# Matrix-memory heads of a two-block network: low parts in the other 64 rows, scores as two rounded products

## The chip, the cores and the metric

The kernel runs on one core of a Trainium2 chip. The metric is the time of one execution on the device in microseconds (us); the time given is the median of the runs shown. The engines are PE (TensorE; PEld is its weight load), DVE (VectorE), ACT (ScalarE), POOL (GpSimd) and SP (SyncE).

## The reference, cut to what matters

Two transformer-like blocks run one after the other on 512 tokens of width 1024. The change lies in the second block, in the matrix-memory heads (mLSTM) of its mixer. There are M_HEADS = 4 heads, with queries and keys of M_DK = 64 and values of M_DV = 128 features:

```python
u_c = jax.nn.silu(causal_dwconv(u, conv_w, conv_b))
u_h = u_c.reshape(Bn, S, M_HEADS, M_DV)
q_m = jnp.einsum('bshd,hde->bhse', u_h, wq_m)      # 64 features a head
k_m = jnp.einsum('bshd,hde->bhse', u_h, wk_m)
...
qk = jnp.einsum('bhcjd,bhcsd->bhcjs', qc, kc) * Dw  # scores times decay
num = (... + jnp.einsum('bhcjs,bhcse->bhcje', qk, vc))
den = (... + jnp.sum(qk, axis=-1))
h = num / jnp.maximum(jnp.abs(den), jnp.exp(-m_j))[..., None]
...
return jnp.concatenate([y_m, y_a], axis=-1) @ w_out
```

The other half of the mixer, y_a, is a causal attention over low-rank queries and keys ("latent attention"), which the kernel runs right behind the heads.

## The kernel before

All engines have programs of their own, written out by hand in the order in which they run; semaphores tie them together. Large products (a "panel" is a group of output columns) are computed from rounded parts: each f32 operand is a rounded high part and a rounded low part of type fp32r, and three rounded products (high·high, high·low, low·high) go into one PSUM bank (lines 410, 486, 2585, 2569). POOL and ACT split the weights (lines 3257, 3265, 1446), a panel ahead of PE. PE's banks 0 to 3 go round: before PE writes block `blk` it waits until the semaphore acc_free has counted block `blk - 4` as read out.

The heads take their place in this order. In the second block PE computes the low-rank panel L_low, then four blocks in which it makes queries and keys of one head each (line 2585, three products of 512 columns: rows 0 to 63 of the bank are the queries, rows 64 to 127 the keys, one column a token), then the value panel L_vb (line 486). ACT copies each bank out in two copies of 64 rows (lines 2713 and 2714), into QM and KM in f32, two heads to a tensor, the even head in the upper 64 rows and the odd head in the lower. The second copy frees the bank. Then ACT goes on with squares, root and scaling of the low-rank tensors (2438, 2444, 2450, 2452), and DVE with its part of them (2457 and 2459).

A head's scores are taken over all 128 rows, since its keys share their tensor with the neighbour head's. So the queries must be zero in the neighbour's 64 rows: POOL makes Q_PADDED with four multiplications by a column mask (`heads_query_pool`, line 2919), between the last weight split ahead of it and `memory_pool`. While it does, DVE computes the gate rows of 4 partitions (`gate_rows_dve`, lines 2397 to 2402), for whose end PE waits at line 2625.

The scores themselves (`mlstm_qk_pe`, line 2649): for key block bs of 0 to 3 (128 keys), PE multiplies the keys with the queries of tokens bs·128 to 511, that is 512, 384, 256 and 128 columns, as one f32 product, which the trace shows as two passes. The results alternate between two banks. DVE multiplies each with its decay block E (line 2795, `ml["w"]`), and PE may write score block u only when DVE has done block u - 2. Between the pairs of blocks PE runs the value products of the head before (line 2663) and the broadcast of the decay row of the head after the next (line 2672); DVE runs the additions of the mask (2678) and the outputs (2804 to 2813). After head 3 comes the latent attention (line 1599), which has products over 128 and over 64 rows.

## Time and profile before

| | |
|---|---|
| median of 3 runs | 1868.13 us (1868.02 to 1868.85) |
| span of the profiled execution | 1866.1 us |
| PE busy | 1836.2 us, 98% |
| PEld busy | 1552.8 us, 83% |
| POOL busy | 1367.8 us, 73% |
| DVE busy | 920.0 us, 49% |
| ACT busy | 756.6 us, 41% |

The profiled execution gives times within its span; the rest of the time, 2.0 us against the median, lies around it. The busy shares are means over many stages. Start times below are from the span's start: the heads' queries and keys are made at 1230 us, the scores at 1304 to 1324 us.

### The profile page before, as it was taken

To read this page: it belongs to the slowest core of one execution; us is meant where nothing else is said; L and a number is where in the kernel's file an instruction comes from. 1 tells how busy PE (TensorE), PEld (TensorE's weight loads), DVE (VectorE), ACT (ScalarE), POOL (GpSimd) and SP (SyncE) were. 2 spreads that over 40 slices of the span, in tenths; PEclk is the share of its full clock that TensorE was granted. 3 is DMA by queue.
4 is the path that set the end of the run, shared out by engine and by line. 5 is a ranking of instruction groups with operands and counts; after the bars stand their busy time and mean duration, and the time that the engine had idled before them with its cause. 6 is when DMAs were issued, how large, how long until landed. Compare 5 with 4: busy or idle time off the path is not lost.

```text
span 1866.1 us, 26050 instructions
## 1 busy us (share of the span) xinstructions
PE 1836.2 (98%) x9519; PEld 1552.8 (83%) x9519; DVE 920.0 (49%) x1806; ACT 756.6 (41%) x1459; POOL 1367.8 (73%) x1211
## 2 busy tenths in 40 slices
PE   7999999999999999999999999999999999999999
PEld 6888888888878888888888888897679988888887
DVE  5677777772117885455403411727664465203410
ACT  4577777764027773242101210567644532001200
POOL 8766666698854558989888988763345589888885
PEclk9999999999999999999999999999999999999999
DMA  7322222223333232422333333222023223432342
GB/s 223 113 69 68 68 69 68 69 68 91 91 114 89 52 86 91 160 68 90 90 105 98 90 93 110 69 63 68 24 68 114 91 68 90 110 93 90 94 109 68
DMA packets 213612, 165.69 MB, mean 89 GB/s; under 512 B 14478, under 2 KB 209873, under 8 KB 213122
## 3 DMA queue, kind: packets, MB, share of 16 engines
q1 hardware_dynamic: 208134, 149.32, 27.3%
q10 hardware_dynamic: 5372, 14.98, 2.4%
q8 instruction: 64, 1.05, 0.2%
q14 instruction: 42, 0.34, 0.1%
HBM read 161.11 MB, written 7.37 MB: 90 GB/s over the span
## 4 chain that ended last, share of the span: by engine, by line
PE 57%; POOL 3%; issue 2%; DVE 2%; ACT 2%; POOLq 0%; ACTq 0%; DVEq 0%
PE bank L410 44%; PE bank L486 4%; POOL w_lo L3265 2%; PE bank L436 1%; PE bank L1599 1%; POOL w_hi L3257 1%; PE bank L3014 1%; PE bank L1623 1%; PE bank L1821 1%; PE bank L1800 1%; PE bank L1810 0%; PE bank L2663 0%; PE bank L1609 0%; PE bank L429 0%; POOL x_features L761 0%
## 5 line engine op out<-in xcount | busy, mean ns | idle before, releaser
L3265 POOL TENSOR_TENSOR w_lo<-w_raw,w_hi 128x512 fp32r<-128x512 f32 (+1 forms) x572 | 721.7, 1294 | 197.9 <-ACT w_hi L1446 188.4
L3257 POOL TENSOR_TENSOR w_hi<-w_raw,one 128x512 fp32r<-128x512 f32 (+1 forms) x428 | 440.8, 1061 | 213.6 <-PE bank L410 193.9
L410 PE MATMUL bank<-h_hi,w_hi 128*128 128x512 f32 x952 | 376.8, 396 | 0.8 <-POOL w_lo L3265 0.6
L410 PE MATMUL bank<-h_hi,w_lo 128*128 128x512 f32 x952 | 371.8, 391 | 0.0
L410 PE MATMUL bank<-h_lo,w_hi 128*128 128x512 f32 x952 | 371.1, 390 | 0.0
L410 PE MATMUL bank<-a_hi,w_hi 128*128 128x512 f32 x832 | 325.8, 392 | 0.4 <-DVE a_lo L553 0.3
L410 PE MATMUL bank<-a_hi,w_lo 128*128 128x512 f32 x832 | 324.0, 389 | 0.0
L410 PE MATMUL bank<-a_lo,w_hi 128*128 128x512 f32 x832 | 323.7, 389 | 0.0
L410 PEld LDWEIGHTS bank<-h_hi,w_lo 128*128 128x128 f32 x952 | 178.6, 188 | 38.9
L410 PEld LDWEIGHTS bank<-h_hi,w_hi 128*128 128x128 f32 x952 | 178.9, 188 | 35.6 <-issue 1.4
L410 PEld LDWEIGHTS bank<-h_lo,w_hi 128*128 128x128 f32 x952 | 179.0, 188 | 33.5
L410 PEld LDWEIGHTS bank<-a_hi,w_hi 128*128 128x128 f32 x832 | 156.2, 188 | 33.0 <-issue 0.6
L410 PEld LDWEIGHTS bank<-a_hi,w_lo 128*128 128x128 f32 x832 | 156.1, 188 | 32.8
L410 PEld LDWEIGHTS bank<-a_lo,w_hi 128*128 128x128 f32 x832 | 156.3, 188 | 31.5
L2174 ACT ACTIVATE arena<-bank 128x512 f32<-128x512 f32 x64 | 38.0, 597 | 319.7 <-PE bank L410 312.9
L2195 DVE TENSOR_TENSOR a_lo<-arena,a_hi 128x512 fp32r<-128x512 f32 x64 | 81.6, 1275 | 156.5 <-ACT a_hi L2166 156.5
L486 PE MATMUL bank<-w_hi,h_hi 128*128 128x256 f32 (+1 forms) x448 | 129.4, 289 | 0.2
L486 PE MATMUL bank<-w_lo,h_hi 128*128 128x256 f32 (+1 forms) x448 | 126.5, 282 | 0.0
L486 PE MATMUL bank<-w_hi,h_lo 128*128 128x256 f32 (+1 forms) x448 | 126.4, 282 | 0.0
L1140 DVE SCALAR_TENSOR_TENSOR arena<-bank,cols,arena 128x510 f32<-128x510 f32 (+1 forms) x128 | 95.6, 747 | 7.7 <-ACT arena L1124 4.3
L486 PEld LDWEIGHTS bank<-w_hi,h_hi 128*128 128x128 f32 x448 | 85.9, 192 | 1.2 <-DVE a_free_hi L2340 0.6
L486 PEld LDWEIGHTS bank<-w_hi,h_lo 128*128 128x128 f32 x448 | 85.9, 192 | 0.3 <-issue 0.2
(506 smaller groups left out, 3012.6 us busy)
## 6 DMA issues: line engine op xcount, KB each, us to landing
w_raw<-in_w_ff SPq DMA_DIRECT2D x32, 1024.0 KB, 5.4
w_raw<-in_w_in SPq DMA_DIRECT2D x31, 1024.0 KB, 5.4
w_raw<-in_w_mlp_in SPq DMA_DIRECT2D x16, 1024.0 KB, 5.3
w_raw<-in_w_mlp_out SPq DMA_DIRECT2D x16, 1024.0 KB, 5.7
w_raw<-in_w_in SPq DMA_DIRECT2D x26, 512.0 KB, 4.1
w_raw<-in_w_ssd_out SPq DMA_DIRECT2D x8, 1024.0 KB, 5.6
bias_rows<-bias_row ACTq DMA_DIRECT2D x1, 4096.0 KB, 15.1
w_raw<-in_w_attn_out SPq DMA_DIRECT2D x4, 1024.0 KB, 5.3
```

Source lines behind the costliest of these rows:

```text
L410: mm = pe.matmul(bank[:, 0:ntok], a, b[:, koff + k, 0:ntok], start=(k == 0 and n == 0), stop=(k == L.kb - 1 and n == 2))
L436: mm = pe.matmul(banks[blk % 4][:], a, b[:, koff + k, :], start=(k == 0 and n == 0 and not ready_high), stop=(k == L.kb - 1 and n == len(p ...
L486: mm = pe.matmul(banks[blk % 4][:, t * width:(t + 1) * width], a[:, k, tok], b, start=(k == 0 and n == 0), stop=(k == L.kb - 1 and n == 2))
L1140: ins = dve.scalar_tensor_tensor(dst[:, lo:hi], src[:, lo + s:hi + s], colv(f"conv_w{k}", conv_column(g, b)), dst[:, lo:hi], ALU.mult, ALU ...
L1599: mm = pe.matmul(score_bank[n % 2][:, 0:w["n"]], qT, kT, start=(i == 0), stop=(i == len(w["q"]) - 1))
L1623: mm = pe.matmul(value_bank[:, 0:dv], mem[1][n % 2][:, j * P:(j + 1) * P], w["v"][j], start=(j == 0), stop=(j == nb - 1))
L1800: mm = pe.matmul(scores_of[:, 0:(k1 - k0) * P], QS[g % 2][:, r, n * P:(n + 1) * P], KS[g % 2][:, part, k0 * P:k1 * P], start=(part == 0), ...
L1821: mm = pe.matmul(value_bank[:], VSTACK[g % 2][:, k0 + j, :], part[:, j, :], start=(j == i == 0), stop=(j == k1 - k0 - 1 and i == 1))
L2174: act.activation(RL[b % 2], acc(L1, b), ACT.Relu).then_inc(ml_relu, 1)
L2195: dve.tensor_tensor(a_lo[:, b, :], SQR[b % 2], a_hi[:, b, :].bitcast(F32), ALU.subtract).then_inc(ml_lo, 1)
L3257: pool.tensor_tensor(w_hi[:, slot, part], raw[:, slot, part], one[:].broadcast_to([P, n]), ALU.mult).then_inc(split_hi, 1)
L3265: ins = pool.tensor_tensor(w_lo[:, slot, part], raw[:, slot, part], w_hi[:, slot, part].bitcast(F32), ALU.subtract)
```

## The change

The heads' queries and keys are kept rounded, with their low parts beside them. QUERIES and KEYS hold one head to a slice of 128 rows. In an even head QUERIES has the rounded queries in the upper 64 rows and their low part in the lower; KEYS has the rounded keys in both halves; the low part of the keys lies in the upper rows of LOW_ROWS. In an odd head the roles of queries and keys are exchanged, and the upper and lower rows of LOW_ROWS with them. ACT makes three copies a head instead of two, DVE two subtractions from the bank, and DVE's second one frees the bank. A score block is then two rounded products into one bank: the first over 128 rows (high·high and one high·low at once), the second over 64 rows (the other one). POOL's four multiplications and the semaphore `padded` go. ACT gets a wait for acc_free ahead of the first read of L_vb.

```diff
-        QM = A(0, 1024).rearrange("p (b s) -> p b s", b=2)
-        KM = A(1024, 1024).rearrange("p (b s) -> p b s", b=2)
+        QUERIES = arena_rounded[:, 0:2048].rearrange("p (h s) -> p h s", h=M_HEADS)
+        KEYS, LOW_ROWS = moving[:, 0:M_HEADS, :], moving[:, M_HEADS:M_HEADS + 2, :]
+        TOP, BOTTOM = slice(0, 64), slice(64, P)
...
-        Q_PADDED = a_free_hi[:, 0:M_HEADS, :]
...
+        def heads_high_act(act, h):
+            bank = banks[(L_low.b0 + T // 2 + h) % 4]
+            act.wait_ge(acc_ready, L_low.b0 + T // 2 + h + 1)
+            if h % 2 == 0:
+                copies = ((QUERIES[TOP, h, :], bank[TOP]), (KEYS[BOTTOM, h, :], bank[BOTTOM]), (KEYS[TOP, h, :], bank[BOTTOM]))
+            else:
+                copies = ((KEYS[BOTTOM, h, :], bank[BOTTOM]), (QUERIES[TOP, h, :], bank[TOP]), (QUERIES[BOTTOM, h, :], bank[TOP]))
+            for dst, src in copies:
+                ins = act.activation(dst, src, ACT.Copy)
+            ins.then_inc(ml["high"], 1)
+
+        def heads_low_dve(dve, h):
+            bank = banks[(L_low.b0 + T // 2 + h) % 4]
+            q_low, k_low = ((QUERIES[BOTTOM, h, :], LOW_ROWS[TOP, h // 2, :]), (LOW_ROWS[BOTTOM, h // 2, :], KEYS[TOP, h, :]))[h % 2]
+            dve.wait_ge(ml["high"], h + 1)
+            dve.tensor_tensor(q_low, bank[TOP], QUERIES[TOP, h, :].bitcast(F32), ALU.subtract)
+            dve.tensor_tensor(k_low, bank[BOTTOM], KEYS[BOTTOM, h, :].bitcast(F32), ALU.subtract).then_inc(acc_free, 1)
...
         def mlstm_qk_pe(pe, h, part):
-            pe.wait_ge(ml["padded"], h + 1)
+            if h == 0 and part[0] == 0:
+                pe.wait_ge(acc_free, L_low.b0 + T // 2 + M_HEADS)
...
-                pe.matmul(QK_RING[u % 2][:, 0:S - bs * P], KM[:, h // 2, bs * P:(bs + 1) * P], Q_PADDED[:, h, bs * P:S],
-                          start=True, stop=True).then_inc(ml["qk"], 1)
+                dst, keys = QK_RING[u % 2][:, 0:S - bs * P], slice(bs * P, (bs + 1) * P)
+                if h % 2 == 0:
+                    low = LOW_ROWS[TOP, h // 2, keys], QUERIES[TOP, h, bs * P:S]
+                else:
+                    low = KEYS[BOTTOM, h, keys], LOW_ROWS[BOTTOM, h // 2, bs * P:S]
+                pe.matmul(dst, KEYS[:, h, keys], QUERIES[:, h, bs * P:S], start=True, stop=False)
+                pe.matmul(dst, *low, start=False, stop=True).then_inc(ml["qk"], 1)
...
             for h in range(M_HEADS):
-                act.wait_ge(acc_ready, L_low.b0 + T // 2 + h + 1)
-                p0 = 64 * (h % 2)
-                act.activation(QM[p0:p0 + 64, h // 2, :], acc(L_low, T // 2 + h, 0, 64), ACT.Copy)
-                act.activation(KM[p0:p0 + 64, h // 2, :], acc(L_low, T // 2 + h, 64, P), ACT.Copy).then_inc(acc_free, 1)
+                heads_high_act(act, h)
             low_rank_squares_act(act, [(4, 128, CKT[:, :, 0:128]), (8, 64, CKT[:, :, 128:192])])
             low_rank_root_act(act)
+            act.wait_ge(acc_free, L_vb.b0)
...
             conv_dve2(dve)
+            for h in range(M_HEADS):
+                heads_low_dve(dve, h)
             low_rank_dve(dve)
...
-        def heads_query_pool(pool):
-            pool.wait_ge(acc_free, L_low.b0 + T // 2 + M_HEADS)
-            pool.wait_ge(lt["turn"], 6)
-            pool.wait_ge(lt["red"], 4 * T)
-            for h in range(M_HEADS):
-                rows = (m_lt[:, 64:65], m_gt[:, 63:64])[h % 2].bitcast(F32)
-                pool.tensor_tensor(Q_PADDED[:, h, :], QM[:, h // 2, :], rows.broadcast_to([P, S]), ALU.mult).then_inc(ml["padded"], 1)
...
-                    heads_query_pool(pool)
                     memory_pool(pool)
```

On ACT, at the place where the banks of the four heads are read out, this stood before (arena stands for QM and KM):

```order
L2424 ACTIVATE arena<-bank,small 128x192
L2713 ACTIVATE arena<-bank 64x512 [waits acc_ready]
L2714 ACTIVATE arena<-bank 64x512
L2713 ACTIVATE arena<-bank 64x512 [waits acc_ready]
L2714 ACTIVATE arena<-bank 64x512
```

And this stands there now (arena_rounded is QUERIES, decay_moving is KEYS and LOW_ROWS):

```order
L2444 ACTIVATE arena<-bank,small 128x192
L2381 ACTIVATE arena_rounded<-bank 64x512 [waits acc_ready]
L2381 ACTIVATE decay_moving<-bank 64x512 x2
L2381 ACTIVATE decay_moving<-bank 64x512 [waits acc_ready]
L2381 ACTIVATE arena_rounded<-bank 64x512 x2
```

Each head has one copy more, and none of the three frees the bank. On DVE, behind the convolution of the second block, these rows are now between the last split of the convolution and the reciprocal of the low-rank part, which stood next to each other before:

```order
L2231 TENSOR_TENSOR a_lo<-arena,a_hi 128x512 [waits sp_hi,ms_uc] x2
L2389 TENSOR_TENSOR arena_rounded<-bank,arena_rounded 64x512 [waits ms_high]
L2390 TENSOR_TENSOR decay_moving<-bank,decay_moving 64x512
L2389 TENSOR_TENSOR decay_moving<-bank,arena_rounded 64x512 [waits ms_high]
L2390 TENSOR_TENSOR decay_moving<-bank,decay_moving 64x512
```

The second subtraction of a head frees its bank. On PE, heads 0 and 1 of the scores read like this before (2672 is the broadcast of the decay row, 2663 a value product):

```order
L2672 MATMUL bank<-arena,ident 128x512
L2649 MATMUL bank<-a_free_hi,arena 128x512 [waits ms_padded]
L2649 MATMUL bank<-a_free_hi,arena 128x384
L2649 MATMUL bank<-a_free_hi,arena 128x256 [waits ms_w,ms_padded]
L2649 MATMUL bank<-a_free_hi,arena 128x128 [waits ms_w]
L2672 MATMUL bank<-arena,ident 128x512 [waits ms_exp]
L2649 MATMUL bank<-a_free_hi,arena 128x512 [waits ms_w,ms_padded]
L2649 MATMUL bank<-a_free_hi,arena 128x384 [waits ms_w]
L2663 MATMUL bank<-arena 128x129 [waits ms_w,lt_kept]
```

And now:

```order
L2698 MATMUL bank<-arena,ident 128x512
L2675 MATMUL bank<-arena_rounded,decay_moving 128x512 [waits acc_free]
L2676 MATMUL bank<-arena_rounded,decay_moving 128x512
L2675 MATMUL bank<-arena_rounded,decay_moving 128x384
L2676 MATMUL bank<-arena_rounded,decay_moving 128x384
L2675 MATMUL bank<-arena_rounded,decay_moving 128x256 [waits ms_w]
L2676 MATMUL bank<-arena_rounded,decay_moving 128x256
L2675 MATMUL bank<-arena_rounded,decay_moving 128x128 [waits ms_w]
L2676 MATMUL bank<-arena_rounded,decay_moving 128x128
L2698 MATMUL bank<-arena,ident 128x512 [waits ms_exp]
```

Each f32 product has become a product over 128 rows (2675) and one over 64 (2676) into the same bank; the rest of PE's order is the same.

## Rows read from the trace of the kernel before

**Rows 1.** The page: span, and busy time of each engine with its share.
```profile
span 1866.1 us, 26050 instructions
PE 1836.2 (98%) x9519; PEld 1552.8 (83%) x9519; DVE 920.0 (49%) x1806; ACT 756.6 (41%) x1459; POOL 1367.8 (73%) x1211
```

**Rows 2.** Busy time by stretches: PE, PEld, DVE, ACT, POOL, clock, DMA.
```profile
1304.20:1323.79 19.59, 18.33 (x97) 12.87 (x96) 12.96 (x41) 12.45 (x41) 0.00 (x0) 1.00 0.00 1
1300.00:1866.00 566.00, 557.46 (x2809) 460.40 (x2807) 218.34 (x432) 155.38 (x341) 397.78 (x326) 1.00 0.28 84
```

**Rows 3.** Timeline, making of queries and keys (PE): start, duration, instruction.
```profile
1232.94 0.39 PE L2585 MATMUL bank<-a_hi,w_lo 128*128 128x512 f32 x1
1233.16 0.28 PE L486 MATMUL bank<-w_hi,h_hi 128*128 128x256 f32 x1
1233.28 0.28 PE L486 MATMUL bank<-w_hi,h_lo 128*128 128x256 f32 x1
```

**Rows 4.** Timeline, the same place on ACT, and where its part ends.
```profile
1231.30 0.59 ACT L2713 ACTIVATE arena<-bank 64x512 f32<-64x512 f32 x1
1231.91 0.60 ACT L2714 ACTIVATE arena<-bank 64x512 f32<-64x512 f32 x1
...
1242.85 1.27 ACT L2452 ACTIVATE arena<-arena,latent_stats 128x128 f32<-128x128 f32 x4
```

**Rows 5.** Groups by shape, DVE: busy us, mean ns; idle before.
```profile
L2195 DVE TENSOR_TENSOR a_lo<-arena,a_hi 128x512 fp32r<-128x512 f32 x64 | 81.6, 1275 | 156.5 <-ACT a_hi L2166 156.5
L1852 DVE TENSOR_TENSOR a_hi<-bank,a_hi 64x512 fp32r<-64x512 f32 x16 | 11.0, 689 | 5.5 <-ACT a_hi L1843 5.1
L2231 DVE TENSOR_TENSOR a_lo<-arena,a_hi 128x512 fp32r<-128x512 f32 x4 | 2.7, 685 | 0.8 <-ACT a_hi L2226 0.8
```

**Rows 6.** Timeline, POOL's padded copies and the gate rows on DVE.
```profile
1287.43 1.21 DVE L2397 TENSOR_TENSOR_SCAN a_free_lo<-a_free_hi,cmask 4x512 f32<-4x512 f32 x1
1288.68 1.35 DVE L2398 TENSOR_TENSOR a_free_lo<-a_free_lo 4x512 f32<-4x512 f32 x1
1290.06 1.95 DVE L2399 TENSOR_TENSOR_SCAN arena<-a_free_lo 4x512 f32<-4x512 f32 x1
1293.42 1.15 DVE L2401 TENSOR_SCALAR arena<-arena 4x512 f32<-4x512 f32 x1
...
1288.39 1.09 POOL L2919 TENSOR_TENSOR a_free_hi<-arena,m_lt 128x512 f32<-128x512 f32 x1 [3.39 <-PE bank L2545]
1292.81 1.48 POOL L2919 TENSOR_TENSOR a_free_hi<-arena,m_gt 128x512 f32<-128x512 f32 x1
```

**Rows 7.** Weight loads of PE around its wait for the gate rows.
```profile
1293.61 0.19 PEld L486 LDWEIGHTS bank<-w_lo,h_hi 128*128 128x128 f32 x1
1294.73 0.32 PEld L2625 LDWEIGHTS bank<-ident,a_free_lo 4*128 4x128 f32 x4 [0.93 <-issue]
```

**Rows 8.** Timeline of the scores: weight loads, PE and DVE.
```profile
1304.63 0.19 PEld L2649 LDWEIGHTS bank<-a_free_hi,arena 128*128 128x128 f32 x1 [0.24 <-issue]
1305.06 0.19 PEld L2649 LDWEIGHTS bank<-a_free_hi,arena 128*128 128x128 f32 x1 [0.24 <-issue]
...
1304.83 0.69 DVE L2678 TENSOR_TENSOR a_free_lo<-bank,a_free_lo 128x512 f32<-128x512 f32 x1 [6.48 <-PE bank L2672]
1305.76 1.20 DVE L2795 SCALAR_TENSOR_TENSOR arena<-bank,arena 128x512 f32<-128x512 f32 x2 [0.24 <-PE bank L2649]
...
1316.26 0.89 PE L2649 MATMUL bank<-a_free_hi,arena 128*128 128x256 f32 x4 [0.44 <-DVE a_free_hi L2795]
...
1320.73 1.03 PE L2663 MATMUL bank<-arena,a_free_hi 128*128 128x129 f32 x6 [0.51 <-ACT a_free_lo L2763]
```

**Rows 9.** Weight loads in the latent attention, 128 and 64 rows in turn.
```profile
1358.92 0.30 PEld L1599 LDWEIGHTS bank<-a_free_lo,a_free_hi 128*128 128x128 f32 x2
1359.98 0.29 PEld L1599 LDWEIGHTS bank<-a_free_lo,a_free_hi 64*128 64x128 f32 x2 [0.76 <-issue]
1361.04 0.14 PEld L1609 LDWEIGHTS bank<-ident,a_free_hi 128*128 128x128 f32 x1 [0.76 <-issue]
```

More of the change, by code:

```diff
@@ L2281, in build_program @@
         MEMB = A(2048, 2048)
-        ml = {k: sem("ms_" + k) for k in ("gates", "rows", "rows_in", "conv", "uc", "qk", "act", "dve", "pe", "arg", "exp", "w", "num", "out", "sq", "inverse", "padded", "bc", "head", "ss", "root")}
+        ml = {k: sem("ms_" + k) for k in ("gates", "rows", "rows_in", "conv", "uc", "qk", "act", "dve", "pe", "arg", "exp", "w", "num", "out", "sq", "inverse", "high", "bc", "head", "ss", "root")}
         lt = {k: sem("lt_" + k) for k in ("ang", "sin", "table", "ss", "root", "inverse", "low", "kr", "red", "qn", "kn", "turn", "kept")}
```

## The prediction

> **What bounds the kernel now.** First the page: PE is busy 98% of 1866.1 us, and no other engine more than 83% [rows 1]. Then the busy time by stretches: from 1300 us to the end PE has 557.46 of 566 us, so what reaches PE's order ahead of that stays in the end time nearly one for one [rows 2]. PE's granted clock is 1.00 in both stretches, the level of 2.4 GHz. The question is therefore only: by how much does each edit move PE? Three places can: where the heads' banks are read out (1231 us), where PE waits for DVE's gate rows (1294 us), and the scores (1304 to 1324 us), where PE is busy 18.33 of 19.59 us [rows 2].
>
> **Place 1, the banks.** Before, PE goes from the last product of the heads (start 1232.94) to the first one of L_vb (1233.16) with no gap; a product of 512 columns lasts 0.22 us from start to start [rows 3]. That first product of L_vb must wait until the bank of head 0 is free. ACT starts on it at 1231.30 and frees it with its second copy at 1231.91 + 0.60 = 1232.5, 0.65 us ahead of the need [rows 4]. Now ACT makes three copies of the same shape at 0.61 us from start to start: 1231.30 + 2 × 0.61 + 0.59 = 1233.1. Then DVE subtracts twice. The trace has a subtraction of this kind, 64 rows by 512, one operand in a bank and one in SBUF: 0.689 us [rows 5]. Two in a row take about 0.60 + 0.69 (the pair of decay products, 1.20 us for 512 and 384 columns, shows such an overlap [rows 8]). DVE is free there; the bank is free at 1233.1 + 0.1 + 1.3 = 1234.5. PE waits from 1233.16 to 1234.5: **+1.35 us**. Bounds: 0 would need subtractions that start before the copies end, which their order excludes; +2.6 if each subtraction takes 1.28 us, as the one with both operands in SBUF does beside POOL [rows 5]. I take 1.35, since the nearest row has the same shape and operand places. The banks of heads 1 to 3 are asked for one 5.8-us block later each, or are never late.
>
> ACT's four extra copies are 2.45 us, less the 1.35 us by which PE is later too. Queued behind them are squares, root and scaling of the low-rank part, whose end releases PE's transposes at 1250 us. That end is at 1242.85 + 1.27 = 1244.1 [rows 4]; even 2.5 us more leaves over 3 us. DVE's reciprocal waits for ACT's root, so the 5 us of subtractions are done long before. ACT's added wait for all four banks is over at about 1240.0, while ACT gets to it at about 1243. All three cost nothing as long as that slack stands.
>
> **Place 2, POOL's copies go.** They run from 1288.39 to 1292.81 + 1.48 = 1294.3, and POOL then waits over 40 us for other things, so POOL gains nothing. But beside them DVE's gate rows are slow: an addition of 4 × 512 takes 1.35 us, the second scan 1.95 where the first, nearly through before POOL began, took 1.21 [rows 6]. Line 2231, a subtraction with two SBUF operands, has 0.685 with POOL idle, where line 2195 has 1.275 [rows 5]. With POOL still I expect 0.68 + 1.25 + 0.68 + 0.65 from 1288.7: the chain ends at about 1292.0 instead of 1294.6. PE waits for it: its last load of the panel is at 1293.61 and the next at 1294.73, with 0.93 us idle [rows 7]. Without the wait the load would still be about 0.13 late, since it has another row count (place 3 has its price). What is late next is PE itself. **-0.80 us**; the bounds are 0 (4-row operations slow for a reason of their own) and -0.93. The Trainium skill (SBUF — State Buffer, SBUF: two separate sides) says that a VectorE instruction with two SBUF inputs and a GpSimd one that reads SBUF lock each other out for the whole instruction. By it the two subtractions at place 1, with an operand in a bank, stay at 0.69 beside POOL's splits, and the trace's rows agree.
>
> **Place 3, the scores.** Before: each f32 product is two passes; for 512 columns a pass takes 1305.06 - 1304.63 = 0.43 us [rows 8], so a head (1280 columns) has 2 × 0.43 × 2.5 = 2.15 us. After: rounded products start 0.22 us apart for 512 columns and 0.12 for 256 [rows 3]; with 0.17 and 0.11 for 384 and 128 between and below them that is 0.62 twice, 1.24 us a head. By streaming alone PE saves 0.91 us a head, 3.6 us in all. But the second product is over 64 rows. The latent attention alternates 128 and 64 rows in just this way [rows 9]. There two f32 passes of 512 columns need 0.86 us, while the loads that begin such a pair come at 1358.92, 1359.98 and 1361.04, 1.06 us apart: each change of the row count costs 1.06 - 0.86 = 0.20 us. The loads show how: a load of the same row count comes a pass ahead (1304.63 for the pass at 1305.06), one of another count only after the pass before is through, with 0.76 us of idle PEld before it. So each score block has two changes, 0.40 us, where PE has no wait to hide them.
>
> The Trainium skill (TensorEngine Tiling (Array Packing), Tiling Modes) states that changing the tiling mode drains the engine. By it each of the 32 changes costs; without it place 3 gains (rival B).
>
> Where they are hidden follows from who waits. Head 1 is all PE: 1.24 + 8 × 0.20 - 2.15 = +0.69. In heads 2 and 3, PE waits for DVE ahead of the third block (0.44 us at 1316.26, and 0.51 for squares of ACT in head 3 [rows 8]), and DVE's chain there starts from the last value product, so what the first two blocks gain or lose falls into that wait. Behind it come blocks of 256 and 128 columns: before 0.43 + 0.22 = 0.65, after 2 × 0.12 + 2 × 0.11 + 4 × 0.20 = 1.26, so +0.61 each. In head 0 the first block is ready sooner, but DVE is at the mask addition until 1304.83 + 0.69 = 1305.52 and starts 0.2 us sooner than 1305.76 [rows 8]; then the same +0.61: +0.4. Sum 0.4 + 0.69 + 0.61 + 0.61 = **+2.3 us**. The bounds are -0.7 (no cost for a change: then only DVE's earlier starts count, some 0.2 in head 0, 0.3 in head 1 and 0.1 in each of the others) and +3.2 (a product of 128 columns that takes a full f32 pair's 0.22 us instead of 0.11, which no row of rounded type shows). I take 2.3, since rows 9 are the same engine doing the same alternation. The removed waits for `padded` were met long before.
>
> **Sum.** +1.35 - 0.80 + 2.3 = +2.85 us. Against the profiled execution: span 1866.1 + 2.85 = 1868.95; 2.0 us lie around it, as before; so 1868.13 + 2.85 = **1871.0 us**, 0.15% more. A measurement of this kernel tells about 0.2%, 3.7 us, from no change, so this counts as no change. The chances below are for faster or slower by more than that.
>
> **Rivals.**
> A, my forecast, with all three terms near their values: 1870.2 to 1871.8.
> B, the changes of row count cost nothing, since a rounded weight load is shorter or comes ahead where an f32 pair does not: +1.35 - 0.80 - 0.7 = -0.15, 1868.0 us. For it: rows 9 are f32 passes only. Against it: their load has the same 0.19 us, or 0.29 for two, as all others.
> C, the subtractions are slowed by POOL's split of the next panel, which starts at 1233.5: each takes 1.28 us and PE waits 2.6 us at place 1. +2.6 - 0.8 + 2.3 = +4.1, 1872.2 us, slower by more than the bound; it decides from about 1.15 us a subtraction. Against it: 0.689 us for the same form in sixteen instructions [rows 5].
> D, the gate rows don't get faster, or PE finds another wait behind them: +3.65, 1871.8 us, at the edge. Against it: the durations in rows 6, long for exactly as long as POOL's copies last.
> E, PE has the gain of 3.6 us in full, because it is PE and not DVE that is late in every head and the row changes are free: +1.35 - 0.8 - 3.6 = -3.05, 1865.1 us, still within the bound. Against it: PE's waits for DVE in rows 8.
>
> **How the numbers follow.** A 0.52, B 0.15, C 0.10, D 0.12, E 0.03, and 0.08 for something that I don't see, either way. Only C, the upper end of A and D, and part of the rest pass 1871.9: slower 0.18. Faster needs 1864.4: 0.04. Same 0.78. The range from B to C, with 0.2 us beyond each end for the spread of the runs, is 1867.8 to 1872.4.
>
> **What would show it.** In the profile after: PE's first product of L_vb about 1.35 us later than its predecessor's end, with DVE as releaser; DVE's subtractions at 0.69 us; the gate rows at 0.7 and 1.2 us and no wait of PE behind them; in the scores, PEld of 64 rows with idle time before each and starts of 128-row and 64-row loads of one block 0.42 us apart for 512 columns (0.22 if B holds); and 21.9 us instead of 19.6 from the first score load to the first load of the latent attention. I am wrong if that stretch is shorter than before, or if PE gets new waits behind 1236 us, where ACT's later squares could be seen.

## The result, and the profile after

The changed kernel took 1871.43 us (median of 20 runs, 1870.52 to 1874.52), the kernel before, beside it, 1868.56 us (20 runs, 1866.75 to 1870.78). The ratio is 1.0016, with a 95% interval from 1.0010 to 1.0023: 2.87 us more, less than the 0.2% taken beforehand as the bound of "the same". The forecast was 1871.0 us, 2.85 us more than the 1868.13 us of the three runs known then; the difference is met to 0.02 us, the time itself to 0.43. One later execution of the kernel before took 4744.11 us and is left out of all that follows.

The page of the changed kernel, the lines that answer to [rows 1]:

```profile
span 1871.0 us, 26051 instructions
...
PE 1840.0 (98%) x9519; PEld 1554.9 (83%) x9519; DVE 923.3 (49%) x1814; ACT 759.1 (41%) x1463; POOL 1361.9 (73%) x1207
```

PE makes the same number of products. That it is busy 3.8 us longer here doesn't measure the change, since both profiles have stretches at half clock: a second profile of the same kernel (after_again, below) has 1836.0 us. DVE has eight instructions more, ACT four more, POOL four fewer. The execution behind this page took 1872.7 us, some 1.3 us above the median, so it has something in it that the median has not. That turns up at place 3.

**Place 1, the banks.** The timeline of PE, DVE and ACT (start, duration, instruction, in brackets the idle time before it and who ended it), to be held against [rows 3, 4]:

```profile
1233.04 0.39 PE L2605 MATMUL bank<-a_hi,w_lo 128*128 128x512 f32 x1
1234.68 0.39 PE L486 MATMUL bank<-w_hi,h_hi 128*128 128x256 f32 x1 [1.26 <-DVE decay_moving L2390]
...
1233.24 0.69 DVE L2389 TENSOR_TENSOR arena_rounded<-bank,arena_rounded 64x512 fp32r<-64x512 f32 x1 [13.16 <-ACT decay_moving L2381]
1233.94 0.69 DVE L2390 TENSOR_TENSOR decay_moving<-bank,decay_moving 64x512 fp32r<-64x512 f32 x1
...
1231.40 0.59 ACT L2381 ACTIVATE arena_rounded<-bank 64x512 fp32r<-64x512 f32 x1
1232.01 1.82 ACT L2381 ACTIVATE decay_moving<-bank 64x512 fp32r<-64x512 f32 x3
```

Before, 0.22 us passed from the start of the last product of the heads to the first one of L_vb; now it is 1234.68 - 1233.04 = 1.64 us. PE is 1.42 us later, and the releaser is DVE's second subtraction of head 0. The chain reads off in order: ACT's three copies from 1231.40, DVE from 1233.24, its end at 1234.63, PE at 1234.68.

**Place 2, the gate rows.** DVE's rows at 1290 us, and PE's weight loads behind them, to be held against [rows 6, 7]:

```profile
1289.08 1.21 DVE L2417 TENSOR_TENSOR_SCAN a_free_lo<-a_free_hi,cmask 4x512 f32<-4x512 f32 x1
1290.33 0.68 DVE L2418 TENSOR_TENSOR a_free_lo<-a_free_lo 4x512 f32<-4x512 f32 x1
1291.04 1.21 DVE L2419 TENSOR_TENSOR_SCAN arena<-a_free_lo 4x512 f32<-4x512 f32 x1
1292.29 0.68 DVE L2420 TENSOR_TENSOR a_free_hi<-a_free_lo,arena 4x512 f32<-4x512 f32 x1
1293.00 0.41 DVE L2421 TENSOR_SCALAR arena<-arena 4x512 f32<-4x512 f32 x1
...
1295.25 0.19 PEld L486 LDWEIGHTS bank<-w_lo,h_hi 128*128 128x128 f32 x1
1295.58 0.32 PEld L2645 LDWEIGHTS bank<-ident,a_free_lo 4*128 4x128 f32 x4
```

The chain that took 1.35 + 1.95 + ... + 1.15 us beside POOL's copies is now 0.68, 1.21, 0.68, 0.41. It ends at 1293.41, some 2 us before PE wants it. From load to load PE needs 0.33 us where it needed 1.12, so 0.79 us are won.

**Place 3, the scores.** For this stretch I show first a second profile of the same kernel (the run after_again below), since its granted clock is 1.00 in all of the stretch, as before. Weight loads of head 3 and the stretch as a window (length, then busy time of PE, PEld, DVE, ACT, POOL, then the clock):

```profile
1320.48 0.19 PEld L2675 LDWEIGHTS bank<-arena_rounded,decay_moving 128*128 128x128 f32 x1
1320.92 0.18 PEld L2676 LDWEIGHTS bank<-decay_moving 64*128 64x128 f32 x1 [0.25 <-issue]
1321.35 0.19 PEld L2675 LDWEIGHTS bank<-arena_rounded,decay_moving 128*128 128x128 f32 x1 [0.25 <-issue]
1321.71 0.18 PEld L2676 LDWEIGHTS bank<-decay_moving 64*128 64x128 f32 x1 [0.18 <-issue]
...
1323.57 0.19 PEld L2675 LDWEIGHTS bank<-arena_rounded,decay_moving 128*128 128x128 f32 x1
1323.88 0.18 PEld L2676 LDWEIGHTS bank<-decay_moving 64*128 64x128 f32 x1
1324.19 0.19 PEld L2675 LDWEIGHTS bank<-arena_rounded,decay_moving 128*128 128x128 f32 x1
1324.45 0.18 PEld L2676 LDWEIGHTS bank<-decay_moving 64*128 64x128 f32 x1
1324.70 1.64 PEld L2689 LDWEIGHTS bank<-arena,a_free_hi 128*128 128x128 f32 x14
...
1305.06:1326.26 21.20, 20.16 (x98) 13.37 (x96) 13.44 (x41) 12.44 (x41) 0.00 (x0) 1.00 0.00 1
```

From the first score load to the first load of the latent attention it is 21.20 us, against 19.59 [rows 2]: +1.61. The loads mark the changes: 0.43 us from one to the next for a product of 512 columns, 0.36 for 384, 0.31 for 256, 0.25 for 128, each with another row count than the one before it. A rounded product of 512 columns without such a change takes 0.22 [rows 3].

In the profiled execution of the changed kernel itself the same stretch has one thing more. The loads of the value products in head 2, and the window over them:

```profile
1318.96 3.08 PEld L2689 LDWEIGHTS bank<-arena,a_free_hi 128*128 128x128 f32 x14
...
1319.00:1322.00 3.00, 3.00 (x16) 3.00 (x15) 0.30 (x2) 0.55 (x3) 0.00 (x0) 0.50 0.00 0
```

The fourteen loads take 3.08 us where they take 1.64 in the other profile. The granted clock is 0.50, the level of 1.2 GHz, and PE is busy without a gap: not a wait, but the same work at half the pace. Those loads lose 1.44 us by it, and the whole stretch, from 1305.05 to 1327.85 in this profile, is 22.80 us, 1.60 more than at full clock. Before, the clock in this stretch was 1.00 [rows 2].

**The sum, from the profiles.** 1.42 - 0.79 + 1.61 = 2.24 us at full clock. From the start of the last product of the heads to the last output DMA's issue it is 630.77 us before (1232.94 to 1863.71) and 633.16 in the full-clock profile: 2.39, so the three places hold all but 0.15 us. This distance is used below to compare kernels, called **the tail** of the kernel; it leaves out what differs by chance ahead of 1232 us.

### The profile page after: what moved, and what is told of

It is laid out like the page before. It is cut to its first block, busy times and chain, and to the rows that moved or that the text cites. A ratio compares the mean times of both kernels' runs of the same rounds, so it can differ in the third digit from the quotient of the medians.

```text
span 1871.0 us, 26051 instructions
## 1 busy us (share of the span) xinstructions
PE 1840.0 (98%) x9519; PEld 1554.9 (83%) x9519; DVE 923.3 (49%) x1814; ACT 759.1 (41%) x1463; POOL 1361.9 (73%) x1207
## 4 chain that ended last, share of the span: by engine, by line
PE 57%; POOL 3%; issue 2%; ACT 2%; DVE 1%; POOLq 0%; ACTq 0%; DVEq 0%
PE bank L410 43%; PE bank L486 4%; POOL w_lo L3281 2%; PE bank L436 1%; PE bank L1599 1%; POOL w_hi L3273 1%; PE bank L3031 1%; PE bank L1623 1%; PE bank L1821 1%; PE bank L2689 1%; PE bank L1800 1%; PE bank L1810 0%; PE bank L1609 0%; PE bank L429 0%; POOL x_features L761 0%
```

## The experiments

Each kernel is the changed kernel with one edit, unless it says "from the kernel before". The runs fall into three groups, each on one chip with its own runs of the kernel before: experiments 1 to 4 (its median there 1868.68 us), experiments 5 to 7 (1868.74), and the repeats bank_again and zeros_again (1868.93).

**1. The row count of the second product (rows128).**

```diff
-                pe.matmul(dst, *low, start=False, stop=True).then_inc(ml["qk"], 1)
+                pe.matmul(dst, KEYS[:, h, keys], QUERIES[:, h, bs * P:S], start=False, stop=True).then_inc(ml["qk"], 1)
```

> The changed kernel, but the second product of each score block repeats the first over all 128 rows instead of the low product over 64, so the scores are wrong and only their time is read. Theory (changes between 128 and 64 rows cost PE about 0.1 to 0.2 us each): the stretch from the first score load to the first load of the latent attention falls from 22.80 us to under 20 us, since it loses the row changes (1.8 us without the slow clock in the profiled run) and nearly 1 us more that the faster products then give; the time falls by 2.5 to 3 us, to about 1868.7. The idle times of PEld ahead of second products are gone. Rival (the row count costs nothing, PE is held by DVE or by the slower clock alone): the stretch stays at 21.4 us or more at full clock and the time at 1871.

1868.42 us (10 runs), ratio 0.9999 [0.9990, 1.0009]; tail 630.54. Head 0's loads, and the window:

```profile
1304.98 0.19 PEld L2675 LDWEIGHTS bank<-arena_rounded,decay_moving 128*128 128x128 f32 x1 [0.24 <-issue]
1305.41 0.19 PEld L2676 LDWEIGHTS bank<-arena_rounded,decay_moving 128*128 128x128 f32 x1 [0.24 <-issue]
1305.64 0.19 PEld L2675 LDWEIGHTS bank<-arena_rounded,decay_moving 128*128 128x128 f32 x1
1305.87 0.19 PEld L2676 LDWEIGHTS bank<-arena_rounded,decay_moving 128*128 128x128 f32 x1
1306.95 0.19 PEld L2675 LDWEIGHTS bank<-arena_rounded,decay_moving 128*128 128x128 f32 x1 [0.90 <-DVE arena L2821]
...
1304.98:1323.65 18.67, 16.18 (x98) 12.69 (x97) 12.96 (x41) 12.31 (x41) 0.00 (x0) 1.00 0.00 1
```

With the same number of products and columns, all over 128 rows, the stretch is 18.67 us instead of 21.20. So the 64 rows, and not the number of products, make place 3 longer: 2.53 us for 32 changes and what follows from them. The window shows a second thing. Against before PE is busy 2.15 us less (18.33 to 16.18), but the stretch is only 0.92 us shorter. The rest has become waiting for the other two engines, whose work has not shrunk (DVE 12.96 us both times). PE waits 1.6 us for ACT's squares (line 2787) and 1.0 us for DVE, where after_again has 0.6 and 0.3; the last load shown comes after 0.90 us of idle time, in the changed kernel after 0.37.

**2. Who frees the bank (bank_by_act).** ACT's third copy frees it. DVE subtracts a head's rounded rows from themselves, so the low parts are zero, and its signal `high` is what PE's first score waits for.

```diff
-            ins.then_inc(ml["high"], 1)
+            ins.then_inc(acc_free, 1)
...
-            dve.wait_ge(ml["high"], h + 1)
-            dve.tensor_tensor(q_low, bank[TOP], QUERIES[TOP, h, :].bitcast(F32), ALU.subtract)
+            dve.wait_ge(acc_free, L_low.b0 + T // 2 + h + 1)
+            dve.tensor_tensor(q_low, QUERIES[TOP, h, :].bitcast(F32), QUERIES[TOP, h, :].bitcast(F32), ALU.subtract)
...
```

> The changed kernel, but ACT's third copy frees the bank, and DVE's two subtractions read only what ACT has written in SBUF, so both low parts are zero; only the time is read. Theory (PE waits 1.3 us for the bank of head 0 because it is freed behind DVE): the first product of L_vb follows the last one of the heads with no gap, everything behind comes 1.4 us earlier, the time is about 1870.0. Rival (L_vb is held by something else, such as its weights): the gap of 1.26 us stays. The subtractions have two SBUF operands now: beside POOL's split I expect some of them at about 1.3 us instead of 0.69, which costs nothing.

1871.23 us (10 runs, 1868.6 to 1874.02), ratio 1.0015 [1.0005, 1.0024], which alone tells nothing of the wait. The timeline of PE does:

```profile
1232.03 0.39 PE L2605 MATMUL bank<-a_hi,w_lo 128*128 128x512 f32 x1
1232.25 0.38 PE L486 MATMUL bank<-w_hi,h_hi 128*128 128x256 f32 x1
```

0.22 us from start to start again, and the tail is 631.71, 1.45 us shorter than the full-clock tail of the changed kernel. The scores keep their 21.21 us. DVE's subtractions, which now have both operands in SBUF, take 0.69 to 1.14 us beside POOL's split instead of 0.69 each; 1.3 was expected for some. Why the median did not follow is not shown; the clock is the likely reason, since 4 of the 10 runs had a mean clock of 0.997 or less, and the only one with 0.999 took 1868.60 us. So the kernel was run again with the third group.

> The kernel whose banks are freed by ACT's third copy, with both low parts zero, once more: its first median, 1871.2, was no better than the changed kernel's although its profile, at full clock, showed the bank's wait gone and 1.6 us less behind it. If the slow clock did that, the runs with a mean clock of 0.999 or more lie at about 1869 to 1870 and those at 0.997 or less over 1871; if the wait gone is worth nothing, the runs at full clock lie at 1871 as those of the changed kernel.

1869.68 us (11 runs), ratio 1.0008 [0.9999, 1.0017]; tail 631.71 again; one run of 11 with the low clock. That is 0.75 us more than the kernel before beside it, where the changed kernel had 2.87 and 2.85 more than its own neighbour. As expected, the seven runs with a clock of 0.999 or more lie at 1869.1 to 1870.2 us and the one with 0.997 at 1872.43. The wait for the bank is worth its length: by the tail 1.45 us, by the medians some 2.

**3. POOL's copies back (pool_back).** POOL copies again, from the rounded queries, into a buffer that nobody reads; PE waits for `padded` as before.

```diff
-            if h == 0 and part[0] == 0:
-                pe.wait_ge(acc_free, L_low.b0 + T // 2 + M_HEADS)
+            pe.wait_ge(ml["padded"], h + 1)
...
+                pool.tensor_tensor(a_free_hi[:, h, :].bitcast(F32), QUERIES[:, h, :].bitcast(F32), rows.broadcast_to([P, S]), ALU.mult).then_inc(ml["padded"], 1)
...
```

> The changed kernel with POOL's four multiplications and PE's waits for them put back at their old place (they read the new queries, and nobody uses what they write). Theory (POOL's copies slow DVE's gate rows, for which PE waits): the gate rows take 1.35, 1.95, 1.35 and 1.15 us again instead of 0.68, 1.21, 0.68 and 0.41, PE waits 0.8 us at the turn of the gate rows, the time is about 0.7 us longer than that of the changed kernel, 1872.1. Rival (the gate rows became faster for another reason, or PE's wait is not worth its length): PE starts the scores no later than in the changed kernel.

1874.19 us (6 runs), ratio 1.0030 [1.0018, 1.0042]. DVE, POOL and PE's load at place 2:

```profile
1289.36 1.35 DVE L2418 TENSOR_TENSOR a_free_lo<-a_free_lo 4x512 f32<-4x512 f32 x1
1290.74 1.95 DVE L2419 TENSOR_TENSOR_SCAN arena<-a_free_lo 4x512 f32<-4x512 f32 x1
1292.71 1.35 DVE L2420 TENSOR_TENSOR a_free_hi<-a_free_lo,arena 4x512 f32<-4x512 f32 x1
...
1290.12 1.49 POOL L2944 TENSOR_TENSOR a_free_hi<-arena_rounded,m_gt 128x512 f32<-128x512 f32 x1
1291.57 1.95 POOL L2944 TENSOR_TENSOR a_free_hi<-arena_rounded,m_lt 128x512 f32<-128x512 f32 x1
...
1295.41 0.32 PEld L2645 LDWEIGHTS bank<-ident,a_free_lo 4*128 4x128 f32 x4 [0.94 <-issue]
```

The long durations come back with the copies and only with them, on both engines, and so does PE's wait: 1295.41 - 1294.28 = 1.13 us from load to load against 0.33. The copies cost 0.80 us through DVE. The median says more than that, +2.8 against the changed kernel (0.7 was expected), but three of the six runs had the low clock, and in the profile a half-clock stretch of some 10 us lies in the scores, with another 3.4 us behind them:

```profile
1308.50:1311.50 3.00, 3.00 (x5) 0.91 (x3) 1.09 (x3) 1.96 (x7) 0.00 (x0) 0.50 0.00 0
```

So the 0.80 rests on the timeline, not on the median.

**4. The change's gain without its costs (zeros_by_dve, from the kernel before).** It computes what the kernel before does. ACT copies the queries straight into the padded buffer, now 64 rows of `moving_free` (an f32 view of the memory that later holds the decay products), and DVE sets the other rows to zero at 1219 us, where it has time. POOL's copies go.

```diff
-        Q_PADDED = a_free_hi[:, 0:M_HEADS, :]
+        Q_PADDED = moving_free[:, 0:M_HEADS, :]
...
-                act.activation(QM[p0:p0 + 64, h // 2, :], acc(L_low, T // 2 + h, 0, 64), ACT.Copy)
+                act.activation(Q_PADDED[p0:p0 + 64, h, :], acc(L_low, T // 2 + h, 0, 64), ACT.Copy)
...
+                ins = dve.memset(Q_PADDED[q0:q0 + 64, h, :], 0.0)
...
```

> The kernel before, computing the same in full, but the padded queries are made without POOL: ACT's first copy of a head writes straight into its 64 rows of a padded tensor, and DVE writes the zeros of the other rows in its idle time behind the convolution. Scores are f32 products over 128 rows as before. It has the change's one gain without its two costs. Theory: no wait for the bank of head 0, gate rows at 0.7 and 1.2 us, PE's wait of 0.8 us there gone, scores as before in 19.6 us; the time is 0.7 us less than before, 1867.9, and 3.5 less than that of the changed kernel. Rival (POOL's copies cost PE nothing): the time is that of before.

1866.80 us (11 runs), ratio 0.9991 [0.9982, 1.0000].

```profile
1219.49 2.37 DVE L2775 MEMSET moving_free<- 64x512 f32 x4 [0.16 <-issue]
...
1289.98 0.68 DVE L2401 TENSOR_TENSOR a_free_hi<-a_free_lo,arena 4x512 f32<-4x512 f32 x1
...
1292.96 0.19 PEld L488 LDWEIGHTS bank<-w_lo,h_hi 128*128 128x128 f32 x1
1293.28 0.32 PEld L2626 LDWEIGHTS bank<-ident,a_free_lo 4*128 4x128 f32 x4
...
1302.75:1322.29 19.54, 18.46 (x98) 12.77 (x97) 12.97 (x41) 12.44 (x41) 0.00 (x0) 1.00 0.00 1
```

The gate rows are fast, PE has no wait behind them (0.32 from load to load), and the scores keep their 19.54 us. Tail 629.97, 0.80 less than before: place 2 alone. In the third group it ran again.

> The kernel with zeros written by DVE once more, to know its time: the first comparison gave 1866.8 against 1868.7 us, 1.9 less, while its profile accounts for 0.8 less between the last product of the heads and the last output transfer. If the profile is the measure, this gives 1867.9 or 0.8 less than before; if the first comparison is, 1866.8. No run should have a mean clock of 0.997 or less.

1867.55 us (11 runs), ratio 0.9993 [0.9984, 1.0003], against 1868.93: the medians differ by 1.9 and 1.4 us, both intervals reach to 1.0000 or past it, and the tail (629.91 this time) explains 0.8. It is the fastest kernel of this study in both groups, but below what a measurement tells from no change. The record shows where the rest lies: the medians of the spans alone differ by 1.1 and 0.8 us, and the other 0.8 and 0.6 us are time outside the span. There the kernel with zeros has 1.8 to 2.0 us in each of its 22 executions, the kernel before 2.0 to 2.2 in 43 of 82 and 2.4 to 3.5 in the other 39. What makes this time long in some executions is not known.

**5. Half as many changes (paired).** Both products over 128 rows of a pair of blocks, then both over 64.

```diff
+            low = []
...
-                    low = LOW_ROWS[TOP, h // 2, keys], QUERIES[TOP, h, bs * P:S]
+                    low.append((dst, LOW_ROWS[TOP, h // 2, keys], QUERIES[TOP, h, bs * P:S]))
...
-                pe.matmul(dst, *low, start=False, stop=True).then_inc(ml["qk"], 1)
+            for operands in low:
+                pe.matmul(*operands, start=False, stop=True).then_inc(ml["qk"], 1)
```

> The changed kernel, computing the same in full, with the products of two score blocks in the order 128, 128, 64, 64 rows instead of 128, 64, 128, 64: half the changes of row count, 16 instead of 32, the same products. Theory (each change costs PE about 0.2 us where it isn't waiting, and the share of time in which the array does nothing brings the slow clock): the stretch from the first score load to the first load of the latent attention falls from 21.4 us (without the slow clock) to about 20.0, fewer runs have a mean clock of 0.997 or less (5 of 20 in the changed kernel), the time is 1869.9. Rival (the 64-row products are slow in themselves, changes or not): the stretch stays at 21.4 us.

1872.14 us (11 runs), ratio 1.0018 [1.0009, 1.0027]. This expectation missed: the time did not fall, and 6 of the 11 runs had a mean clock of 0.997 or less, more than the 5 of 20 of the changed kernel and the 1 of 11 of after_again on the same chip. Head 0's loads:

```profile
1305.00 0.19 PEld L2676 LDWEIGHTS bank<-arena_rounded,decay_moving 128*128 128x128 f32 x1 [0.24 <-issue]
1305.43 0.19 PEld L2676 LDWEIGHTS bank<-arena_rounded,decay_moving 128*128 128x128 f32 x1 [0.24 <-issue]
1305.92 0.29 PEld L2678 LDWEIGHTS bank<-arena_rounded,decay_moving 64*128 64x128 f32 x2 [0.30 <-issue]
1307.27 0.19 PEld L2676 LDWEIGHTS bank<-arena_rounded,decay_moving 128*128 128x128 f32 x1 [1.06 <-DVE arena L2823]
...
1309.30:1316.10 6.80, 6.80 (x25) 5.22 (x24) 2.47 (x5) 2.89 (x9) 0.00 (x0) 0.51 0.00 0
```

PE saves changes, but the first block of a pair is finished only with the second, so DVE starts on it 0.17 us later (counted from the broadcast ahead of the head), and at the third block PEld idles 1.06 us for DVE where it was 0.37. In three of the four heads it comes to nothing at full clock: from the broadcast ahead of head 0 to the one ahead of head 1 it is 3.90 us, where the changed kernel has 3.78; from the broadcast ahead of head 2 to its fourteen value loads 4.79, and from there to those of head 3 5.73, against 4.81 and 5.78 in after_again.

Head 1 can't be compared in this way, and it is the head where PE has no wait in which a saving could vanish. The window shows it at half clock: from its broadcast to that of head 2 it is 8.10 us (1308.36 to 1316.46), against 5.81. If 6.8 us at half clock cost 3.4, some 4.7 would be left, an estimate from these two figures, 1.1 less than in the changed kernel. The two runs with a mean clock of 0.999 took 1870.85 and 1871.68 us, against a median of 1871.38 in after_again, so whether fewer changes gain anything at full clock stays open. The rival, 64-row products that are slow in themselves, doesn't fit the loads: the two over 64 rows take 0.29 us together, so the second one comes without delay, as a load of an unchanged row count does (experiment 6 has the same for f32).

**6. The price of a change for f32 (f32_64rows, from the kernel before).** Each head's f32 scores over its own 64 rows, unpadded, no copies on POOL.

```diff
+            rows = slice(64 * (h % 2), 64 * (h % 2) + 64)
...
-                pe.matmul(QK_RING[u % 2][:, 0:S - bs * P], KM[:, h // 2, bs * P:(bs + 1) * P], Q_PADDED[:, h, bs * P:S],
+                pe.matmul(QK_RING[u % 2][:, 0:S - bs * P], KM[rows, h // 2, bs * P:(bs + 1) * P], QM[rows, h // 2, bs * P:S],
...
```

> The kernel before, computing the same in full, with the f32 scores taken over the head's own 64 rows, so that no padded queries are needed and POOL's copies go; 14 changes of row count instead of none. Theory (a change costs the same in f32, and the gate rows are faster without POOL): the gate-row wait is gone (0.8 us), the score stretch grows from 19.59 to about 21.0 us, the time is 1869.3 at full clock. Rival (changes cost only between rounded products): the stretch stays at 19.6 and the time is 1867.9.

1869.12 us (10 runs), ratio 1.0002 [0.9992, 1.0011]. The ends of the stretch, which begins here at the broadcast ahead of head 0, one change, and passes over 64 rows that follow each other:

```profile
1302.32 0.30 PEld L2673 LDWEIGHTS bank<-arena,ident 128*128 128x128 f32 x2
1303.38 0.29 PEld L2650 LDWEIGHTS bank<-arena 64*128 64x128 f32 x2 [0.76 <-issue]
1303.91 0.19 PEld L2650 LDWEIGHTS bank<-arena 64*128 64x128 f32 x1 [0.24 <-issue]
1304.34 0.19 PEld L2650 LDWEIGHTS bank<-arena 64*128 64x128 f32 x1 [0.24 <-issue]
...
1324.09 0.30 PEld L1599 LDWEIGHTS bank<-a_free_lo,a_free_hi 128*128 128x128 f32 x2
```

The pair of passes before the change is followed after 1303.38 - 1302.32 = 1.06 us by the load of the other row count, with 0.76 us of idle PEld: the very figures of [rows 9]. Where the row count stays at 64, the passes are 0.43 us apart, as over 128 rows [rows 8], so it is the change that costs and not the 64 rows. The stretch is 21.77 us against 20.13 before (1303.66 to 1323.79): 1.64 more for 14 changes of which some fall into waits, and the 0.80 of place 2 pays for half of it. Counted from the first score load, as in the expectation, it is 20.71 us against 19.59.

**7. Both edits together, and the changed kernel again (rows128_bank, after_again).**

> Both timing-only edits together: second products repeat the first over 128 rows, and ACT's third copy frees the bank with both low parts zero, so the scores are wrong and only their time is read. It is the bound for a version with rounded scores and none of the two costs. Theory (the costs add): no gap ahead of L_vb, the score stretch 18.7 us as in the kernel with 128 rows, and from the last product of the heads to the last output transfer 629.1 us, 1.6 less than before; the time 1867.0. Rival (they hide each other): no less than either alone.

1867.63 us (10 runs), ratio 0.9995 [0.9986, 1.0004]; tail 629.17. Without the wait for the bank and without changes of the row count, the tail is 1.60 us shorter than before: about -0.8 of place 2 and -0.9 of place 3 are what is left, so the costs are separate and add.

> The changed kernel as it is, beside the kernel before on one chip: 2.9 us more than before, as in the first comparison. In some runs, not in all, the mean granted clock is 0.997 or less, and those are the ones over 1872.5 us; with the slow clock left out the difference is 2.6 us. In the profile the parts at full clock are as in the first profile: 1.26 us of wait for the bank, no wait at the gate rows, 21.4 us of scores.

1871.59 us (11 runs), ratio 1.0016 [1.0007, 1.0025]; the profile with full clock in the scores that is shown above; tail 633.16. The 2.9 us came again (2.85). Two parts of the expectation did not hold: the scores took 21.20 us and not 21.4, and of the three runs over 1872.5 us only one had a mean clock of 0.997 or less, the other two 0.998.

## Why the prediction was right

The sum came out for the reasons that it named, with one term too large and something else in its place.

**Place 1, forecast +1.35, measured +1.42.** The working (three copies at 0.61, two subtractions at 0.60 and 0.69) gave 1234.5; with ACT starting 0.1 us later it was 1234.68. The subtractions took 0.69 each, the second one beside POOL's split, which had started at 1233.57: rival C, at 1.28 us each, is refuted by the two rows. The two subtractions did not overlap by the 0.1 us that I had counted, which is the difference. Undoing the wait took 1.45 us off the tail (experiment 2).

**Place 2, forecast -0.80, measured -0.79**, and 0.80 in the other direction in experiment 3. The rows took 0.68, 1.21 and 0.68 for 0.68, 1.25 and 0.68; rival D is refuted. The last one took 0.41 and not 0.65, which nobody waits for. The forecast that DVE would no longer be the one that is late, and PE itself would be, is what the 0.33 from load to load shows. That is 0.21 more than the 0.12 between the loads ahead of it, the price of a change to 4 rows; the forecast's 0.13 was only the part of it in which PEld is idle. The Trainium skill (SBUF — State Buffer, SBUF: two separate sides) has it that a VectorE instruction with two SBUF inputs and a GpSimd one that reads SBUF shut each other out for the whole instruction. The trace agrees in the rows of experiment 3, where the instructions of both engines are longer (on DVE 1.35 for 0.68), and in the subtractions of place 1: with one operand in a bank they keep their 0.69 beside POOL, and with both in SBUF (experiment 2) they take up to 1.14.

**Place 3, forecast +2.3, measured +1.61 at full clock.** The mechanism was right: a load of another row count doesn't come ahead of the product before it, and each change costs PE 0.20 us for 512 columns (from load to load 0.43 with it, 0.23 without in experiment 1). Rival B and E, with free changes, are refuted by experiment 1: when the changes really are gone, the same kernel has 18.67 us. Its -0.92 against before stands where the forecast had -0.7 for that case. The Trainium skill (TensorEngine Tiling (Array Packing), Tiling Modes) says that a change of the mode drains the engine, and the trace agrees: with the change a load waits for the product before it, without it the load comes ahead.

The step that was off is a size in the sum: the price of a change beside a product of 128 columns. I had taken 0.11 us for the product and added 0.20. The 0.11 is right where the row count stays (experiment 1 has such loads at 1307.41, 1307.52 and 1307.63), but with the changes the loads at 1324.19, 1324.45 and 1324.70 are only 0.26 and 0.25 apart, so a change adds 0.14 there and not 0.20. There are two such products in a head, together 0.11 us a head and 0.44 in all. The other 0.3 us lie in heads 0, 2 and 3, where the waits for DVE and ACT took up a little more than I had given them. By the marks of the fourteen value loads that end each head, the two profiles at full clock differ so:

```
                        before            changed (after_again)   more
first score load        1304.20           1305.06
heads 0 and 1 end       1310.92   6.72    1312.55   7.49          0.77  (forecast 0.4 + 0.69)
head 2                  1316.87   5.95    1318.92   6.37          0.42  (forecast 0.61)
head 3                  1322.23   5.36    1324.70   5.78          0.42  (forecast 0.61)
latent attention        1323.79   1.56    1326.26   1.56          0.00
```

**What made up for it.** With place 3 at 1.61 the three places make 2.24 us, the tail 2.39, and 2.87 was measured. Most of the difference lies behind the last instruction that the forecast looked at. The last output transfer (SyncE) in the two profiles, with its size and the time from issue to landing, before and then changed:

```profile
out_x<-arena SPq DMA_DIRECT2D x1, 128.0 KB, 2.0
...
out_x<-arena SPq DMA_DIRECT2D x1, 128.0 KB, 2.8
```

It is so in every profile of this study: 1.9 to 2.0 us in the four profiles of the kernel before and of those made from it, 2.7 to 2.9 in the eight of the changed kernel and of those made from it, and from that issue to the end of the span 2.3 to 2.4 us against 3.1 to 3.4. The time outside the span goes the other way. The forecast took it as 2.0 us, as before; it is 1.7 us for the changed kernel, and 2.1 in the median for the kernel before (2.0 to 3.5 over 82 executions). Together 2.39 + 0.93 - 0.4 = 2.9 us. Why the last transfer takes longer, and the time outside the span less, no run shows.

TensorE's clock, which the forecast did not have either, adds little to the medians: of the 20 runs, the 12 with a mean clock of 0.999 or more have a median of 1871.23 us, 0.2 below that of all 20. So the forecast of the difference is nearer than its parts deserve, and that is luck: one term was 0.7 too high, and costs of about that size that were not seen stood in its place.

**What would have shown it wrong.** The stretch of the scores was said to go from 19.6 to 21.9 us; it was 21.20, and 22.80 in the profile with the half clock. No new wait of PE appeared behind 1236 us: in the 57 us from there to the gate rows PE is busy 51.83 us before and 51.87 in after_again.

## What to carry to other kernels

Count the changes of the row count among TensorE's products before counting its columns: rounding the scores saved PE 2.15 us of busy time where all products kept 128 rows, and 32 changes, at 0.14 to 0.20 us each where PE had no wait to hide them, made the stretch 2.53 us longer than that and turned the gain into a loss. A copy on GpSimd that nobody waits for can still be on the path, by the VectorE instructions that run beside it; look at their duration with and without it. And when products are put in another order to save PE time, ask which block the next engine gets first: in the three heads that can be compared, half as many changes bought nothing here, since DVE got its first block later and PE waited.

## What the hardware showed that was not expected

**The clock.** The granted clock fell to 0.50 (1.2 GHz) inside the stretch of the scores in three profiles: the changed kernel (3.4 us), pool_back (some 10 us) and paired (6.8 us). In the changed kernel's stretch PE was busy 3.00 of 3.00 us, and in the other two it had no idle time either while it lasted; ahead of it the stretch had PE at 3.80 of 4.00 us busy in pool_back (1304 to 1308 us) and 3.54 of 4.30 in paired. In the profiles of after_again, bank_by_act and bank_again, which have the same products, it did not happen. Over all runs, a mean clock of 0.997 or less was seen in 20 of 69 executions of the kernels whose rounded scores change the row count (after, after_again, bank_by_act, bank_again, pool_back, paired), and in 8 of 135 of the others (before 7 of 83, rows128_bank 1 of 10, rows128, f32_64rows and both runs of zeros_by_dve 0 of 42). The count is an association, and the mean over a whole execution doesn't say where the clock fell. The profile of the kernel before has a mean of 0.997 with 1.00 in its scores; it has its half clock elsewhere:

```profile
1160.00:1170.00 10.00, 10.00 (x51) 8.70 (x50) 2.55 (x5) 1.84 (x3) 6.69 (x7) 0.75 0.35 105
```

Between 800 and 815 us it has 0.89, and the changed kernel's profile has 0.89 and 0.76 in the same two windows. So the half clock comes in other stretches too, whatever the scores are. f32_64rows changes the row count and has none in 10; what brings the drop was not settled. The drop is worth somewhat less than half its length: 1.60 us for 3.4 in the changed kernel's scores.

**Two engines in each other's way.** DVE and POOL held each other up for most of an instruction: 0.68 became 1.35, 1.21 became 1.95, and POOL's own copies 1.49 and 1.95 us where the first of them, begun beside a scan nearly through, had 1.09.
